# A two-block transformer kernel on one core: the gated linear attention writes its outputs with tokens on partitions

## What is computed

```python
def gla_chunked(q, k, v, g, s0):            # per head, chunks of 64 tokens
    b = jnp.cumsum(gc, axis=2)
    q_dec = qc * jnp.exp(b); k_intra = kc * jnp.exp(-b); k_state = kc * jnp.exp(b_last - b)
    scores = jnp.where(mask, einsum('bnthd,bnshd->bnhts', q_dec, k_intra), 0.0)
    o_intra = jnp.einsum('bnhts,bnshv->bnthv', scores, vc)
    def step(S, xs):
        o = jnp.einsum('bthd,bhdv->bthv', qd, S)
        S = S * jnp.exp(bl)[..., None] + jnp.einsum('bthd,bthv->bhdv', ks, vv)
        return S, o
    ...
def gla_output(o, r, out_norm, w_out):
    o = rmsnorm(o, out_norm).reshape(B, L, GLA_HEADS * GLA_DV)
    return (o * jax.nn.silu(r)) @ w_out
```

## Time and profile before

| what | value |
|---|---|
| median of 3 runs | 1344.7 us (1343.38 to 1349.42) |
| the profiled execution's own time | 1344.82 us |
| its span in the trace | 1343.0 us |
| granted TensorE clock, mean | 0.997 |
| PE busy | 1312.4 us (98%) |
| ACT busy | 685.3 us (51%) |
| DVE busy | 584.0 us (43%) |
| POOL busy | 707.9 us (53%) |
| share of PE in the chain that ended last | 93% |

### The profile page before, as it was taken

One profiled execution on the slowest core, in us unless ns is written; L12 is line 12 of the kernel. 1 busy time (PEld: TensorE's weight loads), 2 busy tenths in 40 slices (PEclk: granted clock), 3 DMA queues, 4 the chain that ended last, 5 costly groups with the idle time before them and its releaser, 6 DMA issues.

```text
span 1343.0 us, 22327 instructions
## 1 busy us (share of the span) xinstructions
PE 1312.4 (98%) x8256; PEld 1106.8 (82%) x8256; DVE 584.0 (43%) x1105; ACT 685.3 (51%) x1056; POOL 707.9 (53%) x307
## 2 busy tenths in 40 slices
PE   5999999999999999999999999999999999999999
PEld 1688787777888888888768757999999987999999
DVE  3423686235444443400045565455532485455620
ACT  3561226344444444422236754666665667766652
POOL 0442002352444444454335311698899775798897
PEclk8999999999999999999999999999999999999999
DMA  9433743452433333443435251666666541566664
GB/s 359 172 94 99 252 150 142 148 213 63 173 96 101 101 94 94 132 133 106 161 136 197 101 204 42 237 191 199 189 203 208 179 139 57 188 192 196 191 205 126
DMA packets 60135, 210.20 MB, mean 157 GB/s; under 512 B 6432, under 2 KB 9760, under 8 KB 59936
## 3 DMA queue, kind: packets, MB, share of 16 engines
q1 hardware_dynamic: 59632, 207.52, 47.1%
q10 hardware_dynamic: 432, 1.70, 0.3%
HBM read 208.15 MB, written 1.05 MB: 156 GB/s over the span
## 4 chain that ended last, share of the span: by engine, by line
PE 93%; DVE 2%; ACT 2%; DMA 1%; SPq 1%; issue 1%; ACTq 0%; DVEq 0%
PE ps L338 74%; PE ps L459 2%; PE ps L1097 2%; DMA raw<-wstream 1%; PE ps L1091 1%; PE ps L393 1%; PE ps L1083 1%; PE ps L1437 1%; PE ps L375 1%; PE ps L385 1%; PE ps L1416 1%; SPq L300 1%; PE ps L1419 1%; PE ps L1077 1%; PE ps L1397 1%
## 5 line engine op out<-in xcount | busy, mean ns | idle before, releaser
L327 POOL TENSOR_TENSOR wlo<-raw,whi 128x1024 fp32r<-128x1024 f32 x291 | 695.6, 2409 | 619.8 <-ACT whi L322 619.5
L322 ACT ACTIVATE whi<-raw 128x1024 fp32r<-128x1024 f32 x291 | 306.6, 1056 | 220.6 <-PE ps L338 151.2
L338 PE MATMUL ps<-Hhi_,whi 128*128 128x256 f32 (+1 forms) x1344 | 391.9, 319 | 0.0
L338 PE MATMUL ps<-Hlo_,whi 128*128 128x256 f32 (+1 forms) x1344 | 387.8, 316 | 0.0
L338 PEld LDWEIGHTS ps<-Hhi_,whi 128*128 128x128 f32 x1344 | 252.5, 188 | 23.1 <-issue 4.6
L338 PEld LDWEIGHTS ps<-Hlo_,whi 128*128 128x128 f32 x1344 | 252.4, 188 | 20.2 <-issue 1.9
L338 PE MATMUL ps<-Hhi_,wlo 128*128 128x256 f32 (+1 forms) x1344 | 233.6, 316 | 0.0
L338 PEld LDWEIGHTS ps<-Hhi_,wlo 128*128 128x128 f32 x1344 | 195.9, 188 | 18.4
L338 PE MATMUL ps<-hidhi,whi 128*128 128x256 f32 (+1 forms) x528 | 151.1, 315 | 0.0
L338 PE MATMUL ps<-hidlo,whi 128*128 128x256 f32 (+1 forms) x528 | 150.7, 314 | 0.0
L750 ACT ACTIVATE u<-ps,par 128x256 f32<-128x256 f32 (+1 forms) x132 | 83.9, 636 | 112.1 <-PE ps L338 97.7
(11 more groups left out here) (323 smaller groups left out, 1587.2 us busy)
## 6 DMA issues: line engine op xcount, KB each, us to landing
raw<-wstream SPq DMA_DIRECT2D x375, 512.0 KB, 3.7
Haside<-wstream SPq DMA_DIRECT2D x8, 512.0 KB, 5.7
Paside<-wstream SPq DMA_DIRECT2D x4, 512.0 KB, 4.8
XT<-x_t SPq DMA_DIRECT2D x1, 1024.0 KB, 11.5
XT<-ctx_t SPq DMA_DIRECT2D x1, 1024.0 KB, 13.3
memx<-mem_t ACTq DMA_DIRECT2D x1, 1024.0 KB, 5.4
out_t<-XT SPq DMA_DIRECT2D x1, 640.0 KB, 5.5
par<-params SPq DMA_DIRECT2D x1, 457.5 KB, 3.3
```

The costliest lines, as they stand in the source:

```text
L322: nc.scalar.activation(whi[:, n % RING, :], raw[:, r % RAWS, :], ACT.Copy).then_inc(S["hi_ready"], 1)
L327: nc.gpsimd.tensor_tensor(wlo[:, r, :], raw[:, r, :], whi[:, n % RING, :].bitcast(F32), ALU.subtract).then_inc(S["lo_ready"], 1)
L338: mm = nc.tensor.matmul(o, a, b, start=start, stop=stop)
```

## The change

The stationary and the moving operand of both output groups are exchanged, so that the output of a head gathers with tokens on partitions. `out_rows(tt)` is the 128 tokens of tile `tt`, 256 value columns wide (two tiles per bank, banks 4 and 6).

```diff
-                for vt in range(2):
-                    for tt in range(4):
-                        nc.tensor.matmul(ps[:, OBANK[vt], tt * P:(tt + 1) * P], gv[:, tt, h * 256 + vt * P:h * 256 + (vt + 1) * P],
-                                         am[:, d, tt * P:(tt + 1) * P], start=(d == 0 and tt == 0), stop=False, skip_group_check=True)
+                for tt in range(4):
+                    nc.tensor.matmul(out_rows(tt), am[:, d, tt * P:(tt + 1) * P], gv[:, tt, h * 256:(h + 1) * 256],
+                                     start=(d == 0 and tt % 2 == 0), stop=False, skip_group_check=True)
+                if c in (1, 5):
+                    mod_products(pe, 0, 5 + c if c == 1 else 4 + c)
                 for j in range(1, NCH):
                     ch = ORDER[d][j]
+                    p0 = CH * (ch % 2)
                     pe.wait_ge(S["g_S"], 7 * c + j)
-                    for vt in range(2):
-                        mm = nc.tensor.matmul(ps[:, OBANK[vt], ch * CH:(ch + 1) * CH], Sh[:, j, vt * P:(vt + 1) * P],
-                                              qdec[:, b, ch * CH:(ch + 1) * CH], start=False, stop=(d == 1 and j == NCH - 1), skip_group_check=True)
+                    mm = nc.tensor.matmul(out_rows(ch // 2)[p0:p0 + CH, :], qdec[:, b, ch * CH:(ch + 1) * CH], Sh[:, j, :],
+                                          start=False, stop=(d == 1 and j == NCH - 1), skip_group_check=True)
                 mm.then_inc(S["g_o"], 1)
```

With tokens on partitions a head's statistic is a sum along the free axis. `out_sums`, `add_squares` and DVE's scaling are gone; ACT takes the statistic of every head by itself, and scales while it copies the head out, after `kst` of the next step:

```diff
+            def stats(h):
+                act.wait_ge(S["g_o"], 2 * h + 2)
+                act.wait_ge(S["g_q"], 6 * (h + 1))
+                for tt in range(4):
+                    ins = nc.scalar.activation((gq, gk)[tt // 2][:, h, 256 * (tt % 2):256 * (tt % 2) + 256], out_rows(tt), ACT.Square,
+                                               accum_out=ostat[:, h, tt:tt + 1])
+                alink(ins)
+                alink(log_square(ostat[:, h, :], ostat[:, h, :], 256))
+                alink(inverse_root(ostat[:, h, :]))
+
+            def scaled(h):
+                for tt in range(4):
+                    ins = nc.scalar.activation(out_tokens(h, tt), out_rows(tt), ACT.Copy, scale=ostat[:, h, tt:tt + 1])
+                ins.then_inc(S["g_of"], 1)
```

```diff
+            def out_turns(m):
+                pe.wait_ge(S["g_of"], m // 2 + 1)
+                if m >= 4:
+                    pe.wait_ge(S["g_oc"], m - 3)
+                for tt in range(4):
+                    mm = nc.tensor.transpose(ps[:, m % 4, tt * P:(tt + 1) * P], out_tokens(m // 2, tt)[:, m % 2 * P:m % 2 * P + P], ident)
+                mm.then_inc(S["g_ot"], 1)
...
+            def out_gain(m):
+                act.wait_ge(S["g_ot"], m + 1)
+                if m >= 3:
+                    act.wait_ge(S["g_vec"], m - 2)
+                nc.scalar.activation(gexp[:, m % 3, :], ps[:, m % 4, :], ACT.Copy, scale=pc("g_out", m % 2)).then_inc(S["g_oc"], 1)
```

More of the change, by code:

```diff
@@ L160, in build @@
             names += f" {t}_u {t}_c1 {t}_free {t}_s {t}_hf {t}_hi {t}_pair {t}_dn"
-        names += " z1 gqk gvc g_z g_abs g_l g_zd g_G g_b g_e g_q g_kt g_kst g_sc g_am g_U g_S g_o g_of g_osq g_oss g_orstd g_on g_sr g_vec g_yh g_y go_x"
+        names += " z1 gqk gvc g_z g_abs g_l g_zd g_G g_b g_e g_q g_kt g_kst g_sc g_am g_U g_S g_o g_of g_ot g_oc g_sr g_vec g_yh g_y go_x"
         names += " m_dn m_csq m_css m_cstd m_crv m_cn m_clo m_half m_ev m_qsq m_qss m_qlog m_qrstd m_qn m_ksq m_kss m_klog m_krstd m_kn m_sw m_rot"
@@ L217, in build @@
             posi = sb(part, "posi", [P, T], I32)
+            ostat = sb(part, "ostat", [P, GH, 4])
         with ExitStack() as part:
@@ L992, in build, with out_rows, out_tokens @@
         OBANK = (4, 6)
+        GR_BANK = (5, 4, 6)
+        def out_rows(tt):
+            return ps[:, OBANK[tt // 2], 256 * (tt % 2):256 * (tt % 2) + 256]
+        def out_tokens(h, tt):
+            return of[:, 2 * h + tt // 2, 256 * (tt % 2):256 * (tt % 2) + 256]
         def update(ch):
@@ L1061, in gla_pe @@
                 h, d = divmod(c, 2)
-                if c < 3:
+                if c in (0, 2):
                     mod_products(pe, 0, 5 + c)
@@ L1101, in gla_pe @@
                     mod_turn(pe, 2)
-                elif 3 <= c < 7:
+                elif c in (3, 5, 6):
                     mod_products(pe, 0, 5 + c)
@@ L1105, in gla_pe @@
                     mod_turn(pe, 3)
[L1107 to L1113, removed]
+            def out_turns(m):
[5 more added lines that the diff above has]
+                mm.then_inc(S["g_ot"], 1)
+            for m in range(4):
+                out_turns(m)
             for m in range(8):
                 n = START["gr"] + m
+                if m == 1:
+                    pe.wait_ge(S["g_of"], GH)
                 if m >= 3:
                     pe.wait_ge(S["g_y"], m - 2)
-                column_tile(pe, n, 4 + m % 3, xhi, xlo, TT)
-                if m == 0:
-                    out_sums(GH - 1)
+                if 2 <= m < 6:
+                    out_turns(m + 2)
+                column_tile(pe, n, GR_BANK[m % 3], xhi, xlo, TT)
                 if m == 5:
@@ L1173, in gla_act @@
                 after(c)
+                if c % 2 == 0 and c >= 2:
+                    scaled(c // 2 - 1)
                 if c + 1 < 2 * GH:
@@ L1179, in gla_act @@
                 if c % 2:
[L1180 to L1192, removed]
+                    stats(c // 2)
+            scaled(GH - 1)
+            def out_gain(m):
[3 more added lines that the diff above has]
+                nc.scalar.activation(gexp[:, m % 3, :], ps[:, m % 4, :], ACT.Copy, scale=pc("g_out", m % 2)).then_inc(S["g_oc"], 1)
+            for m in range(3):
+                out_gain(m)
             nc.scalar.preload_act_table(ACT.Silu)
@@ L1196, in gla_act @@
                 act.wait_ge(S["slot_used"], used(n))
-                nc.scalar.activation(ps[:, 4 + m % 3, :], ps[:, 4 + m % 3, :], ACT.Silu).then_inc(S["g_sr"], 1)
-                act.wait_ge(S["g_vec"], GH + m + 1)
-                nc.scalar.activation(yhi[:, m, :], ps[:, 4 + m % 3, :], ACT.Copy).then_inc(S["g_yh"], 1)
+                y = ps[:, GR_BANK[m % 3], :]
+                nc.scalar.activation(y, y, ACT.Silu).then_inc(S["g_sr"], 1)
+                act.wait_ge(S["g_vec"], m + 1)
+                nc.scalar.activation(yhi[:, m, :], y, ACT.Copy).then_inc(S["g_yh"], 1)
+                if m + 3 < 8:
+                    out_gain(m + 3)
                 hi_slot(act, n + RING)
@@ L1274, in gla_dve @@
                     first(1)
-            def add_squares(h):
-                dve.wait_ge(S["g_osq"], 2 * h + 2)
-                nc.vector.tensor_tensor(gq[:, h, :], gq[:, h, :], gk[:, h, :], ALU.add).then_inc(S["g_vec"], 1)
             for c in range(2 * GH):
@@ L1283, in gla_dve @@
                 third(c)
-                if c % 2 == 0 and c >= 2:
-                    add_squares(c // 2 - 1)
                 if c + 1 < 2 * GH:
@@ L1290, in gla_dve @@
             gain_scale(dve, 0, 1, 4)
-            add_squares(GH - 1)
             for m in range(8):
[L1293 to L1297, removed]
+                y = ps[:, GR_BANK[m % 3], :]
+                dve.wait_ge(S["g_oc"], m + 1)
                 dve.wait_ge(S["g_sr"], m + 1)
-                nc.vector.tensor_tensor(y, y, of[:, m, :], ALU.mult).then_inc(S["g_vec"], 1)
+                nc.vector.tensor_tensor(y, y, gexp[:, m % 3, :], ALU.mult).then_inc(S["g_vec"], 1)
                 dve.wait_ge(S["g_yh"], m + 1)
```

## The result

| what | before | with the change |
|---|---|---|
| median, 20 runs each | 1344.29 us (1342.68 to 1350.09) | 1351.14 us (1346.02 to 1354.57) |
| ratio of the undisturbed runs | | 1.0034, 95% interval 1.0022 to 1.0046 |
| the profiled execution | 1344.82 us, span 1343.0 | 1354.46 us, span 1352.7 |
| mean granted clock of it | 0.997 | 0.995 |
| PE busy | 1312.4 us | 1314.6 us |

The kernel is slower by 0.34%, some 4.6 us (3.0 to 6.2 by the interval), which is inside "no change" as the prediction bounded it. Of all the timed runs in this document one is counted as disturbed and stands in no ratio, a run of e7 with 4413.61 us. The two profiled spans differ by 9.7 us.

What follows compares the result with a forecast made beforehand. PE, busy 98% of the span, was taken as the bound. Loop: -11.1 + 3.4 + 1.4 + 7.4 = +1.1 us; with +1.2 after it, +2.3 on 1344.8 gives 1347.0 us, range 1340 to 1352.5.

Steps and rivals of the forecast that it cites:

- signs of being wrong: Checks in the later trace: stalls under 1 us, clock at 0.50 behind one, or a state group over 3 us.
- the length of `out_turns`: After the loop, each set of four transposes was to take 0.59 us, as in the loop.
- PE's work in the output groups: In the loop, both groups fall from 5.05 to 3.66 us a step, saving 11.1 us over 8 steps.
- The states' pace: State groups without a unit ahead wait for DVE's last state, 0.55 to 0.6 us in 6 steps: +3.4 us.
- The waits for `kint`: Scores wait for DVE's `kint` where no unit stands between steps (0 to 1, 4 to 5): 2 x 0.7 = +1.4 us.
- ACT's chain: Behind a head, squares, loads, logarithm and exponential delay `kst`; PE stalls before updates of steps 2, 4, 6: +7.4 us.
- A load with a drain: Rival, slower: ACT empties before each of six loads, 1.4 us more for each; 1355 us, chance 3%.
- The clock: Rival, slower: PE's clock halves in the three stalls, up to 3.4 us each; +10 us, 1357, chance 7%.
- The halves: State products on the array's two halves overlap; the rival, no overlap, loop some 5 us longer, 1352 us, had 6%.
- After the loop: Sums by `ones` go (3.54 us), eight sets of four transposes come (4.72 us): +1.2 us.

Runs made afterwards that it cites:

- e7: The kernel of e1 with every state product sent to the lower half of the partitions; 1344.99 us, ratio 1.0002 to the kernel before.
- e4: The changed kernel with the modulation units put back where they stood before the change; 1347.44 us, ratio 1.0024 to the kernel before.
- e1: The changed kernel with one table set for logarithm and exponential selected before the loop, so its six loads go; 1338.21 us, ratio 0.9963 to before.
- e3: The changed kernel with one more table load per head ahead of its squares; 1353.79 us, ratio 1.0084 to the kernel before.
- e6: The changed kernel, loads kept, with two units placed behind each of steps 1, 3 and 5 and one inside step 0; 1339.94 us, ratio 0.9966 to before.
- e2: The changed kernel with five unused products on PE ahead of its `kst` wait in steps 2, 4 and 6; 1346.8 us, ratio 1.0028 to before.

## Why the prediction was right, and where its sizes were off

The forecast was 1347.0 us with a range of 1340 to 1352.5; the median is 1351.14, and the ratio gives 4.6 us where 2.3 were forecast, less than the interval's lower end of 3.0. Two of its own signs of being wrong came: the clock shows 0.50 behind a stall (twice), and the loop is 5.1 us longer where "within 2 us" was said. Its other signs held but for the length of `out_turns`: PE's waits ahead of steps 2, 4 and 6 (2.6, 2.1, 2.1), six loads of 1.28 with nothing beside them, a state group of 1.9 to 2.3. That the median lies in the range owes something to luck. No term of the sum held the clock; it fell behind two waits of three and for 3.4 us, not three times for 6.8 as the rival priced it, and the profiled execution, 1354.46 us, lies above the range. Its steps, in its own order:

- **PE's work in the output groups**: forecast 3.66 us a step, measured 1.92 + 1.87 = 3.79. The group inside chunks was put at 1.78; the switch from the updates' half-row form was missing in it (the group's first product starts 0.31 us behind the last update, where records inside a group pass every 0.22). 8 x 0.13 = 1.0 us too good.
- **The states' pace**: forecast 0.55 to 0.6 in six steps, measured 2.34 - 1.87 = 0.47, so 2.8 in place of 3.4. The waits for `kint` came where they were forecast, 1.3 us for 1.4. But the scores behind them take 1.13 us where they take 0.89 elsewhere, and from updates to updates such a step is 1.0 us longer than one with a unit, less the unit (e4): 2.0 for 1.4.
- **ACT's chain**: forecast 4.73 us from the squares' start to the end of the statistic, measured 4.74 (squares 1.57 for 1.6, loads 1.28 each). PE's wait was forecast at 7.4 and is 6.8: the link from PE's last product to the first square, put at 0.2 each time, is 0.02. e1, e3 and e6 show it from three sides: take the loads away, add one, cover them.
- **A load with a drain**: it would have added 8 us. In the chain above 0.02 us lie before the first load, and the logarithm begins 0.02 after it; e3's load does the same. The Trainium skill ("ScalarE: Activation LUTs", What ACT_TABLE_LOAD costs) puts a switch at 2.66 us with the drain; the trace shows 1.28 alone. The same page of the Trainium skill (Table sets: the hidden batching unit) says that the logarithm followed by the exponential needs one load, since one set holds both. The changed kernel has two per head, and e1 has none once that set is selected by name: that one set holds both agrees with e1, but here it had to be asked for.
- **The clock**, the rival with 7%: this is the step that was mis-sized. It was treated as all or nothing with a price of up to 3.4 us a fall, and "2.8 is nearer to 1.4" was the reason to leave it out. The clock did fall, behind two of three waits, and e2 puts the price at 2.9 us together. With it and the sizes above, the forecast of the loop goes from +1.1 to +4.4 (1.1 + 1.0 - 0.6 + 0.6 - 0.6 + 2.9); 5.1 is measured. What is left, 0.7, lies in small pieces: 0.14 for each `mod_turn` behind a state group (0.99 us, 0.85 before), 0.16 in unit 5 (2.08 us, 1.92 before), under 0.1 each in the updates behind a wait.
- **The halves** overlap, as forecast; e7 gives the price of the rival, 5.9 us in the loop where 5 were put.
- **After the loop**: forecast +1.2 us, measured +0.2 (51.3 us from the end of the loop to the output projection, 51.1 before). The 0.59 us of four transposes came from a row right behind a unit, where the switch of form is in it. Four sets on end take 1.80, and one between gate tiles 0.44:

```profile
226.93 1.80 PE ps L1124 x16
228.73 10.92 PE ps L339 x48
239.65 0.44 PE ps L1124 x4
```

So the mechanism was the forecast one, PE's work traded against waits behind ACT's chain, but the trade in the loop was not nearly equal: +5.1 us for +1.1. The clock is the largest part of that. With the tail, which was put 1.0 too high, the profile has +5.3 where +2.3 was forecast; the timed runs have +4.6. Where the new program places the units was taken as given in the prediction; e4 to e6 show that it was the second lever.

## What to carry to other kernels

When work is taken off the engine that sets the time, list at each of its waits what the other engines do between the signal and the answer, and compare that with the work that is left as cover: here 4.7 us of ACT and 0.6 for `kst` itself against 3.3 of PE. Then there are two cures, and both worked: shorten the answer (one table set for both functions), or move independent work of the bound engine behind the signal. Loads of activation tables are cheap beside long work and dear in a chain, so look for them in the order of instructions whenever a logarithm and an exponential move into a loop.

## What was not expected of the hardware

**The clock can fall behind a wait of 2.1 us, and need not.** The profiled changed kernel waited 2.6, 2.1 and 2.1 us and had half the clock for 3.4 us behind the first and the third; e4 waited as long, and had it behind the first and the second; e3, with waits of 3.8, 3.4 and 3.4, had it for 6.8 us behind two of three:

```profile
164.90:171.70 6.80, 5.98 (x19) 4.38 (x20) 2.02 (x5) 3.88 (x10) 0.00 (x0) 0.50 0.50 202
188.80:195.60 6.80, 5.91 (x19) 4.35 (x20) 1.96 (x5) 3.91 (x10) 0.00 (x0) 0.50 0.33 132
```

In e6, with waits of 0.9 and less, it kept full clock, and in e2 with 2.3 us of idle products in each wait too. The timed runs agree: the 46 runs of the kernel before beside the experiments have a mean clock of 0.997 (39) or 0.996 (7), those of the changed kernel 0.994 or 0.995 in 9 of 20, and e1, e2 and e6 never less than 0.996. What decides between a fall and none at the same length was not tried.

**A second pace of the split-weight products.** In the up-projection of the second layer one window (columns as above) of the kernel before, then of the changed kernel:

```profile
900.00:980.00 80.00, 80.00 (x708) 80.00 (x707) 41.38 (x90) 55.17 (x89) 70.53 (x30) 1.00 0.62 192
```

```profile
900.00:980.00 80.00, 80.00 (x682) 80.00 (x681) 39.54 (x86) 53.07 (x86) 68.02 (x29) 1.00 0.56 184
```

Same code, same granted clock, PE without a gap in both, and 4% fewer products: 0.118 us each in place of 0.113, over some 135 us, which makes the 5.0 us that the two profiles differ by behind the mixer. e4's profile has it, those of the other seven experiments don't. But the pace is not theirs alone: in the profile before, products of these shapes are 0.118 us apart from 834 to 854 us, at full clock too, and in e1's from 830 to 848. Both are back at 0.113 by 868; what differs is that the changed kernel's profile stays at 0.118 up to 1005. The kernel before has a group of timed runs at 1348 to 1350 us beside its 1342 to 1346, which is that distance; whether they are the same thing no profile shows. It isn't put down to the change, and its cause is open. It may be why medians and single profiles differ here by more than the ratio does.
